# The normed rows of a one-core transformer kernel start 64 bytes lower in SBUF

## What is computed

```python
def rmsnorm(x, g):
    xf = x.astype(jnp.float32)
    y = xf * lax.rsqrt(jnp.mean(xf * xf, axis=-1, keepdims=True) + RMS_EPS)
    return (y * g.astype(jnp.float32)).astype(x.dtype)

def swiglu(h, w13, w2):                     # w13: 1024 x 5632, w2: 2816 x 1024
    g, u = jnp.split(h @ w13, 2, axis=-1)
    return (jax.nn.silu(g) * u) @ w2

for i in range(4):
    x = x + mixer_i(rmsnorm(x, norm_mix_g[i]))
    x = x + swiglu(rmsnorm(x, norm_ffn_g[i]), f_w13[i], f_w2[i])
```

## Time and profile before

| | us |
|---|---|
| median of 3 executions | 2030.51 |
| lowest, highest | 2023.94, 2033.21 |
| the profiled execution, its time | 2043.56 |
| the profiled execution, its span | 2041.8 |

### The profile page before, as it was taken

The page is one execution under the profiler, slowest core; times in us unless marked ns, Lnnn a source line. Parts: engine busy times, 40 slices in busy tenths (PEclk is TensorE's granted clock), DMA queues, the critical chain, the costliest instruction groups (busy, mean ns, idle before and its releaser), DMA issues.

```text
span 2041.8 us, 32534 instructions
## 1 busy us (share of the span) xinstructions
PE 1935.0 (95%) x13424; PEld 1759.5 (86%) x13424; DVE 1374.9 (67%) x1569; ACT 923.0 (45%) x990; POOL 46.3 (2%) x65
## 2 busy tenths in 40 slices
PE   6999998999999979999999999999989999999999
PEld 6998887777777769899989999987878999999998
DVE  4767975766777665766667665567997555675555
ACT  4544843655565553433445443334334333434342
POOL 0000000000000000000101000000000000000000
PEclk8998998999999999999999999999999999999999
DMA  7552341776777747555653375552324555555553
GB/s 223 182 169 86 104 157 71 296 286 254 269 289 293 259 158 201 165 165 186 199 171 125 104 238 191 185 178 91 103 83 146 178 190 187 165 165 165 188 200 106
DMA packets 243915, 366.03 MB, mean 179 GB/s; under 512 B 12566, under 2 KB 217961, under 8 KB 231401
## 3 DMA queue, kind: packets, MB, share of 16 engines
q1 hardware_dynamic: 243817, 364.64, 53.0%
HBM read 363.57 MB, written 1.05 MB: 179 GB/s over the span
## 4 chain that ended last, share of the span: by engine, by line
PE 67%; DVE 15%; DMA 7%; ACT 7%; issue 4%; SPq 0%; DVEq 0%; POOL 0%; ACTq 0%
PE proj L931 36%; PE acc L1265 11%; PE proj L950 8%; DMA raw<-in_w_exp_up_dram 6%; DVE ring_lo L2425 3%; PE proj L1448 2%; DVE ring_lo L3108 2%; ACT ring_hi L1864 2%; ACT ring_hi L2152 1%; ACT second_hi L2152 1%; PE acc L1418 1%; DVE second_lo L3108 1%; PE acc L1524 1%; PE acc L1278 1%; DMA raw<-in_w_in_dram 1%
## 5 line engine op out<-in xcount | busy, mean ns | idle before, releaser
L2425 DVE TENSOR_TENSOR ring_lo<-raw,ring_hi 128x2048 fp32r<-128x2048 f32 x242 | 559.9, 2317 | 228.6 <-ACT ring_hi L1864 227.6
L1864 ACT ACTIVATE ring_hi<-raw 128x2048 fp32r<-128x2048 f32 x242 | 462.1, 1913 | 465.8 <-PE proj L931 214.7
L931 PE MATMUL proj<-h_hi,ring_hi 128*128 128x256 f32 x1808 | 521.3, 288 | 15.2 <-DVE ring_lo L2425 9.6
L931 PE MATMUL proj<-h_lo,ring_hi 128*128 128x256 f32 x1808 | 508.7, 281 | 0.0
L931 PE MATMUL proj<-h_hi,ring_lo 128*128 128x256 f32 x1808 | 508.6, 281 | 0.0
L931 PEld LDWEIGHTS proj<-h_hi,ring_hi 128*128 128x128 f32 x1808 | 343.8, 190 | 28.0 <-issue 14.4
L931 PEld LDWEIGHTS proj<-h_lo,ring_hi 128*128 128x128 f32 x1808 | 344.2, 190 | 4.2 <-issue 3.2
L931 PEld LDWEIGHTS proj<-h_hi,ring_lo 128*128 128x128 f32 x1808 | 345.4, 191 | 0.0
L931 PE MATMUL proj<-g_hi,ring_hi 128*128 128x256 f32 x704 | 197.0, 280 | 4.1 <-DVE hid L2958 4.1
L931 PE MATMUL proj<-g_lo,ring_hi 128*128 128x256 f32 x704 | 196.3, 279 | 0.0
L931 PE MATMUL proj<-g_hi,ring_lo 128*128 128x256 f32 x704 | 196.2, 279 | 0.0
(11 more groups left out here) (440 smaller groups left out, 3429.4 us busy)
## 6 DMA issues: line engine op xcount, KB each, us to landing
raw<-in_f_w_dram SPq DMA_DIRECT2D x132, 1024.0 KB, 5.0
raw<-in_w_exp_gate_dram SPq DMA_DIRECT2D x32, 1024.0 KB, 4.8
raw<-in_w_exp_up_dram SPq DMA_DIRECT2D x32, 1024.0 KB, 5.0
raw<-in_w_exp_down_dram SPq DMA_DIRECT2D x32, 1024.0 KB, 4.8
raw<-in_w_in_dram SPq DMA_DIRECT2D x29, 1024.0 KB, 5.1
raw<-in_a_w_in_dram SPq DMA_DIRECT2D x24, 1024.0 KB, 5.2
raw<-in_b_w_qkv_dram SPq DMA_DIRECT2D x12, 1024.0 KB, 5.1
raw<-in_c_w_in_dram SPq DMA_DIRECT2D x12, 1024.0 KB, 5.1
```

The costliest lines, as they stand in the source:

```text
L931: last = pe.matmul(bank[:, a, :], w[:, k, a * P:(a + 1) * P], h[:, k, :], start=(k == 0 and w is hi and h is h_h and (a == 0 or not first) ...
L1864: act.activation(w_hi[n.slot][:, :], raw[n.slot][:, :], ACT.Copy).then_inc(hi_ready, 1)
L2425: dve.tensor_tensor(w_lo[n.slot][:, :], raw[n.slot][:, :], w_hi[n.slot][:, :].bitcast(f32), SUB)\
```

## The change

Three of the small tiles (`ssq`, `ms`, `neg_half`: 32 + 32 + 64 = 128 bytes) stand ahead of `h_hi`. The other two, `inv` and `eps_col`, go behind `inv_b`. No instruction is added, removed or moved on any engine; only addresses differ.

```diff
@@ -338,15 +338,15 @@
         x = sb("x_res", [P, TT, D])
         ssq = sb("ssq", [P, TT, 2])
         ms = sb("ms", [P, TT])
-        inv = sb("inv", [P, TT])
         neg_half = sb("neg_half", [P, 16])
-        eps_col = sb("eps_col", [P, 1])
         h_hi = sb("h_hi", [P, KT, SEQ], f32r)
         h_lo = sb("h_lo", [P, KT, SEQ], f32r)
         ident = sb("ident_sb", [P, P])
         ones = sb("ones", [P, P])
         params = sb("params", [P, PARAM_TILES * P])
         inv_b = sb("inv_b", [P, SEQ])
+        inv = sb("inv", [P, TT])
+        eps_col = sb("eps_col", [P, 1])
```

## The result

| | before | after |
|---|---|---|
| median (us) | 2029.86 | 2050.9 |
| lowest, highest | 2023.94, 2033.21 | 2045.62, 2051.43 |
| executions | 4 | 4 |
| profiled execution, its time | 2043.56 | 2051.43 |
| profiled execution, its span | 2041.8 | 2049.6 |

The ratio is 1.0101, with a 95% interval of 1.0072 to 1.013. The medians differ by 21.0 us. By the interval the change costs 14.6 to 26.4 us. The two profiled spans differ by 7.8 us only, and the gap between the two figures has to be explained too.

The account below looks back on a forecast made before the run. TensorE, busy 95%, was taken as the bound, through its time per matmul. All terms summed to 0, put on the median of 2030.51 us and shaded to 2029 us; whole range 2010 to 2044 us.

Parts of the forecast that it names:

- the elementwise work: VectorE and ScalarE operations on moved tiles: under 0.1 us over the writes of each half of h, taken as 0.
- the transposes: TensorE's transposes with ident, the first waiting until 6.23 us for its load: taken as 0, plus or minus 0.3 us.
- g's round would stay: Feed-forward part 0, operand g: the round should still take 16.40 us after the change.
- a cadence is entered after a wait and then kept: Line 931: TensorE enters a cadence after a wait and keeps it over hundreds of matmuls; the two are 4.4 ns apart.
- the fifth bullet of the change: The 6384 matmuls of 256 columns on h: the only term that can be large, taken as 0.
- the ends of +6.5 and -20.2 us: Products on h: 1,473 fast matmuls all turning slow, or 4,597 slow ones all turning fast, at 4.4 ns each.
- The reason given for the 0: Line 931: g and h both start 64 bytes over a multiple of 128, yet differ in speed, so address alone doesn't decide.
- The pairs own with ring and own with second: Expert matmuls with stationary own: 404 and 404 ns busy, start gaps within 1.1 ns of 229, read as no alignment effect.
- Rival B: Products on h: moving and weight slices on one 128-byte boundary collide more, 14 to 28 us slower; 0.18 shared with another rival.
- Its hint: Line 950: moving slice from the ring starts at a multiple of 128 and is nearly always slow, 853 of 885 gaps.
- Rival A: Products on h: slice distance from 192 to 128 modulo 256 ends the longer cadence, up to 20.2 us faster; chance 0.32.
- The page's rule: TensorE's independent read ports: a start address could not matter, change worth 0.0 us; the trace was said to agree only half.

Follow-up runs that it names:

- e5: Kernel before with only eps_col moved behind inv_b, so h starts 32 bytes lower and the work region stays: ratio 1.0089.
- e6: Kernel before with neg_half alone ahead of h, the other four small tiles behind inv_b, so h starts 128 bytes lower: ratio 1.0046.

## Why the prediction was wrong

What held: line 931 is the place, its cadence is what a round takes, the other engines don't matter, and the elementwise work, the transposes and the start of the kernel cost nothing. VectorE and ScalarE kept their durations to 1 ns or so. That g's round would stay was right too, in part by luck: in e5 and e6 a loop on g changed its cadence though g had not moved. That a cadence is entered after a wait and then kept, at the same places, was right for most stretches.

**The step that failed is the fifth bullet of the change, the value taken for the 256-column products.** It was priced by "the row that it is nearest to", h unchanged, at 0, with the ends of +6.5 and -20.2 us. Measured, it is between 15 and 24 us. From the first profile of before it is the 15.6 us above. From the two later ones it is more: 5334 gaps of line 931 from 115.2 ns to 119.1 are 20.8 us, and line 950 and line 1448 add 1.4 and 1.0, together 23.2. The medians say 21.0, with 14.6 to 26.4 as the interval, so the time can't tell the two bases apart. Both ends assumed that only the two cadences of the trace exist. There were others, 118.6 and 120.0 ns, longer than both, and the trace of before could not show them, as none of the products on h, g, own or hid had N 128 in it.

**The reason given for the 0 was wrong as well.** The argument ran: g and h both start 64 bytes over a multiple of 128, and one is fast and the other slow, so the address does not decide. It looked at the address of one operand. What counts is the difference of two, and modulo 256, not 128. Under that number g and h are the same case too (N 192), so their contrast could not tell anything about an address. That the loops of h and g differed was the chance of that profile: in two further ones they run alike. The other contrast, of h with itself, fast from 41 to 82 us and slow from 771 to 836, was no chance, as it repeats; but it shows only that one N has two cadences, not that another N has the same two. The pairs own with ring and own with second did differ in N (64 and 0), but they are 512 columns wide, where in the trace of before N 0 and 64 differ by 1.1 ns, and the poor values are others (32, 96, 128 and 192: 232.1 to 233.5 ns). They bounded the wrong thing.

**The rivals.** Rival B had the right kind of event, a longer cadence than the two for every product on h, and had it at 14 to 28 us, with a part in 0.18. Its mechanism is half right. Two streams with the same start modulo 128 are indeed slower, but that is N 0 and 128, two values of eight: at 64, 96, 160 and 224 they are mostly slower than the 113.4 ns of 192 as well, and 32 bytes of shift suffice (e5). Its hint, that line 950 is always slow because its moving slice starts at a multiple of 128, is wrong: line 950 was slow since its N was 64, and it ran at 113.5 ns at 192. Rival A had named the right quantity, the distance modulo 256, from 192 to 128, and gave it the wrong sign.

**The base.** The profiled execution was 13 us above the median, and the prediction noted it and moved on. It was the trace's only sign that the 118 ns loops on h need not be so. Of the slow stretches only these two loops changed in the later profiles; those from 83 to 98 and from 771 to 836 us stayed. On the later base 7.5 us (5334 x 1.4 ns) move from the one end to the other: the gain of 20.2 us shrinks and the loss of 6.5 us grows. Even that end, 14 us, is still made of the two old cadences. So the base is a second, smaller error: h's move to N 128 costs on either base.

**The page's rule** (the Trainium skill, "SBUF — State Buffer", Who interferes with whom: independent read ports for the moving operand and the weight loads, and TensorE waits on no one) would have given 0.0 us. The measurement decides against it in this kernel: moving h or the work region by 64 bytes, or the ring by 192 (with x and the small tiles), changed the time by 0.8 to 1.6%, while moving all tiles by 64 changed it by 0.2%. Whether the two reads collide in SBUF or elsewhere is not shown. That the cadences depend on the difference of their addresses is shown; the cause behind it stays open, and so do the shape of the table and what exactly selects one of the cadences of an N.

## What to carry to other kernels

In this kernel, where TensorE runs matmuls back to back with a weight load each, the relative start of the moving and the stationary slices, modulo 256 bytes, is worth up to 6 ns in 113, and a small tile declared ahead of a large one can change it for thousands of matmuls. In a kernel of this kind, after any edit of the layout, compare a loop round in the timeline with its old length. A cadence read from one profile is one draw: where the profiled execution stands off the median, take another before its stretches are explained. An operation's price is bounded only by rows that share every relation with it, not just its own address.

## What was not expected of the hardware

The same program keeps one of two cadences, 113.4 or 117.8 ns, for a whole loop of nine rounds, and which one differed between profiled executions (16.40 or 16.82 us a round, at a granted clock of 1.00), while other stretches kept theirs in all three. Half of a shift can cost more than the whole: with h_hi alone moved, line 931 has 120.0 ns against 119.1 with both. And the preference depends on the width: N 0 is the worst for line 931, with 256 columns, 119.9 ns, and the best for line 1265, with 512, 227.3.
